# A half tile's matmuls reordered: 16 with the high weights first, 8 with the low weights behind their own wait

## The chip, the core and the metric

The kernel runs on one core of one Trainium2 chip. The metric is the device time of one execution in microseconds; the time of a version is the median of its runs. One further execution was recorded by the hardware profiler, and all rows below come from that one.

## The reference, cut to what matters

One inference step of a decoder layer with 264 tokens (256 of a prompt and 8 single ones), all in float32: a norm, one input projection of 2048 x 7168, convolution and retention heads, an output projection of 2048 x 2048, a second norm, a query projection of 2048 x 2048, a top-16 choice of experts, and then a mixture over all 16384 experts. The two big tables dominate the work:

```python
u = u_tab[idx]
act = jax.nn.gelu(jnp.einsum('td,thkd->thk', xb, u).astype(jnp.float32), approximate=False)
w = (gate * act).astype(xb.dtype)
return jnp.einsum('thk,thkd->td', w, v_tab[idx])
```

The kernel doesn't gather. It multiplies all tokens with the whole of `u_tab` and of `v_tab` and weights each expert by its gate, which is zero for those not chosen.

## The kernel before, in words

**Products in three parts.** Each float32 operand is split into a high part (a cast to the type fp32r) and a low part (the operand less its high part). A product is the sum of three matmuls: high weights with high data, high weights with low data, low weights with high data. The data are 264 columns wide, the tokens.

**Tiles and halves.** All weights are one stream of 344 tiles of 2048 x 128 (in the second table 1024 x 128 pairs), cut into 688 half tiles of 512 KB, each of 8 blocks of 128 x 128. A half tile goes through a ring of 4 slots: SyncE loads it into `raw` (L382), ScalarE casts it to `whi` (L439, semaphore `hi_done`), VectorE subtracts and writes `wlo` (L882, semaphore `lo_done`), and TensorE multiplies in `half` (L629 to L639), 24 matmuls, the last of which counts up `half_used`. SyncE reloads a slot of `raw` when its subtraction is done, and ScalarE casts into a slot of `whi` when TensorE is done with the half tile that was 4 before it.

**The order of the work.** Each engine runs its own list in order, and the lists meet only at semaphores. On ScalarE and VectorE the cast and the subtraction of a tile stand in `ahead(r, k)`, one tile before TensorE's use of it, in among the other work of the stage. The stages are: the first norm (`normalise(0)`, which makes `xhi` and `xlo` two chunks at a time, L921 and L923; TensorE's first tile waits for each two chunks), the heads, the convolution, the output projection, the second norm (`normalise(1)`, the same again), the queries with the top-16 on VectorE (`top16`), the first 8 tiles of `u_tab` (half tiles 176 to 191, beside `route` on VectorE), the gates (batches of 33 small matmuls, L821), and then 16 groups with 16 rounds of 32 half tiles in loops: 8 tiles of `u_tab`, and 8 tiles of `v_tab` with `wexp_hi` and `wexp_lo` as the data.

**What the change and the steps touch.** `half` is called by `tile`, `query_tiles`, `v_tiles` and once for the first tiles of `u_tab`. Its argument `waits` names, for a block c, semaphores that are awaited just before that block's first matmul: after the two norms one wait for each two blocks, for the first output tile one for each block.

Of the kernel before, what the change touches and what calls it, by code (L numbers as in the profile page):

```python
# [41 lines left out]
HALF = 8  # L42
HCOLS = HALF * P
RING = 4
# [118 lines left out]
def build(nc, halves, xT, conv_state, ret_state, norm_mix, conv_w, gn_g, gn_b, norm_ffn, keysT, norm_fin,  # L163
          consts, out_yT, out_conv, out_pret, out_sret):
    with ExitStack() as ctx:
# [3 lines left out]
        def sem(name):  # L169
            return ctx.enter_context(nc.semaphore(name))  # L170
# [137 lines left out]
        hi_done = sem("hi_done")  # L308
        lo_done = sem("lo_done")
# [318 lines left out]
        def _(pe):  # L628
            def half(r, off, out, mh, ml, start, stop, waits=()):  # L629

                s = off % RING
                pe.wait_ge(lo_done, RING * r + off + 1)
                for c in range(HALF):
                    for sem_, need in (waits[c] if c in waits else ()):
                        pe.wait_ge(sem_, need)
                    nc.tensor.matmul(out, whi[:, s, c], mh[c], start=start and c == 0, stop=False)  # L636
                    nc.tensor.matmul(out, whi[:, s, c], ml[c], start=False, stop=False)  # L637
                    mm = nc.tensor.matmul(out, wlo[:, s, c], mh[c], start=False, stop=stop and c == HALF - 1)  # L638
                mm.then_inc(half_used, 1)  # L639

# [6 lines left out]
            def tile(r, k, o4, off, hi_, lo_, waits=({}, {}), between=None):  # L647

                out_free(o4, off)
                b = bank[off % BANKS][:, 0:T]  # L650
                half(r, 2 * k, b, [hi_[:, c, :] for c in range(HALF)], [lo_[:, c, :] for c in range(HALF)],
                     True, False, waits[0])
                if between:
                    between()
                half(r, 2 * k + 1, b, [hi_[:, HALF + c, :] for c in range(HALF)],
                     [lo_[:, HALF + c, :] for c in range(HALF)], False, True, waits[1])
# [113 lines left out]
            def query_tiles(i):  # L770
                first = isinstance(i, int) and i == 0
                for k in range(4):
                    w = norm_waits(CH // 2) if first and k == 0 else ({}, {})
                    if first:
                        pe.wait_ge(x1_ready, CH - BANKS + k + 1)
                    else:
                        pe.wait_ge(q_ready, i * 4 + k - 3)
                    b = bank[k][:, 0:T]
                    r = W_Q // 2 + i * 2
                    half(r, 2 * k, b, [xhi[:, c, :] for c in range(HALF)], [xlo[:, c, :] for c in range(HALF)],  # L780
                         True, False, w[0])
                    if not (first and k == 0):
                        if first and k == 1:
                            pe.wait_ge(keys_in, 32)
                        score(i * 4 + k - 1, (k - 1) % 2)
                    half(r, 2 * k + 1, b, [xhi[:, HALF + c, :] for c in range(HALF)],
                         [xlo[:, HALF + c, :] for c in range(HALF)], False, True, w[1])
# [688 lines left out]
```

## Time and profile before

| | |
|---|---|
| time, median of 3 runs | 2391.52 us (2389.67 to 2396.49) |
| span of the profiled execution, first to last instruction | 2386.3 us |
| median less span | 5.2 us |
| TensorE busy | 2227.3 us |
| matmuls | 20233, of which 16512 in `half` |
| mean granted TensorE clock | 0.963 |

The profiled execution has no time of its own beside its span; the 5.2 us are what lies around the span if it was an execution like the median one. A span is read as a chain: what ended last, and what each piece of it waited for. A matmul's recorded duration overlaps its neighbours', so the pace of TensorE is read from one start to the next.

### The profile page before, as it was taken

What the parts mean: (1) busy time and instruction counts of PE and PEld (TensorE: products, weight loads), DVE (VectorE), ACT (ScalarE), POOL (GpSimd) and SP (SyncE); (2) the same over time, 40 slices, a digit from 0 to 9 for tenths busy, and PEclk for the clock granted to TensorE, in tenths of its full rate; (3) what the DMA queues carried; (4) which work ended last, traced back from release to release, by engine and by line L of the source; (5) the groups of instructions that cost most, each with busy time, mean ns of one, the idle gap of its engine ahead of it and who ended that gap; (6) DMA issues with size and microseconds to landing.
All of it is one profiled execution on the core that took longest, in us unless ns stands there. A gap on an engine that the chain in (4) does not pass through costs nothing.

```text
span 2386.3 us, 52677 instructions
## 1 busy us (share of the span) xinstructions
PE 2227.3 (93%) x20233; PEld 2180.7 (91%) x20233; DVE 1521.5 (64%) x2851; ACT 914.4 (38%) x1162; POOL 33.6 (1%) x55
## 2 busy tenths in 40 slices
PE   4999999997983699999999999999999999999987
PEld 3999899997983699999999999999999999999987
DVE  4566666547789866666666666666666665655554
ACT  2444433332431334344443444434344443333422
POOL 0000000000010000000000000000000000000000
PEclk8999999998996699999999999999999999999999
DMA  3555445553441154545555455454544544555543
GB/s 143 183 171 170 158 151 181 193 174 106 157 135 62 42 171 169 172 165 169 169 168 170 167 169 168 167 171 165 163 168 168 172 165 168 185 179 183 181 135 107
DMA packets 104180, 379.70 MB, mean 159 GB/s; under 512 B 12192, under 2 KB 12464, under 8 KB 103760
## 3 DMA queue, kind: packets, MB, share of 16 engines
q1 hardware_dynamic: 100368, 365.28, 45.9%
q0 software_dynamic: 3648, 11.87, 1.7%
q8 instruction: 148, 2.42, 0.4%
q14 instruction: 16, 0.13, 0.0%
HBM read 370.06 MB, written 6.96 MB: 158 GB/s over the span
## 4 chain that ended last, share of the span: by engine, by line
PE 64%; DVE 5%; issue 2%; DVEq 0%; ACT 0%; ACTq 0%
PE bank L636 21%; PE bank L637 20%; PE bank L638 20%; PE bank L821 3%; DVE gated L1323 1%; DVE wlo L882 1%; DVE gates L1188 1%; DVE gates L1186 0%; DVE acc L1401 0%; PE bank L660 0%; DVE gates L1116 0%; DVE gates L1107 0%; DVE gates L1176 0%; DVE gates L1108 0%; DVE onehot L1314 0%
## 5 line engine op out<-in xcount | busy, mean ns | idle before, releaser
L882 DVE TENSOR_TENSOR wlo<-raw,whi 128x1024 fp32r<-128x1024 f32 x688 | 831.7, 1223 | 656.7 <-ACT whi L439 650.8
L439 ACT CAST whi<-raw 128x1024 fp32r<-128x1024 f32 x688 | 713.1, 1049 | 953.1 <-PE bank L638 931.5
L636 PE MATMUL bank<-xhi,whi 128*128 128x264 f32 x3200 | 928.7, 290 | 48.2 <-DVE xlo L923 21.2
L637 PE MATMUL bank<-xlo,whi 128*128 128x264 f32 x3200 | 914.9, 286 | 0.0
L638 PE MATMUL bank<-xhi,wlo 128*128 128x264 f32 x3200 | 914.5, 286 | 0.0
L636 PEld LDWEIGHTS bank<-xhi,whi 128*128 128x128 f32 x3200 | 610.6, 191 | 65.1 <-issue 50.3
L637 PEld LDWEIGHTS bank<-xlo,whi 128*128 128x128 f32 x3200 | 611.6, 191 | 0.3
L638 PEld LDWEIGHTS bank<-xhi,wlo 128*128 128x128 f32 x3200 | 608.5, 190 | 0.0
L636 PE MATMUL bank<-wexp_hi,whi 128*128 128x264 f32 x2048 | 586.0, 286 | 9.8 <-DVE wexp_lo L1352 9.8
L638 PE MATMUL bank<-wexp_hi,wlo 128*128 128x264 f32 x2048 | 581.6, 284 | 0.0
L637 PE MATMUL bank<-wexp_lo,whi 128*128 128x264 f32 x2048 | 581.0, 284 | 0.0
L636 PEld LDWEIGHTS bank<-wexp_hi,whi 128*128 128x128 f32 x2048 | 386.3, 189 | 10.1 <-issue 9.9
L637 PEld LDWEIGHTS bank<-wexp_lo,whi 128*128 128x128 f32 x2048 | 386.9, 189 | 0.2
L638 PEld LDWEIGHTS bank<-wexp_hi,wlo 128*128 128x128 f32 x2048 | 385.3, 188 | 0.0
L1358 DVE TENSOR_TENSOR acc<-bank,acc 128x264 f32<-128x264 f32 x256 | 100.0, 426 | 68.3 <-PE bank L638 68.3
L821 PE MATMUL bank<-gated,onehot 128*128 128x32 bf16 x3168 | 96.7, 179 | 29.3 <-DVE gated L1323 29.3
L821 PEld LDWEIGHTS bank<-gated,onehot 128*128 128x128 bf16 x3168 | 87.1, 98 | 35.4 <-DVE gated L1323 18.0
L1314 DVE TENSOR_TENSOR onehot<-iota,i2T 128x1408 bf16<-128x1408 bf16 x96 | 84.9, 885 | 0.0
L1323 DVE TENSOR_TENSOR gated<-onehot,stats 128x352 bf16<-128x352 bf16 x288 | 80.6, 335 | 0.0
L636 PE MATMUL bank<-yhi,whi 128*128 128x264 f32 x256 | 75.6, 295 | 0.0
L594 ACT COPY gates<-bank 128x352 f32 x96 | 45.2, 471 | 74.1 <-PE bank L821 74.1
L638 PE MATMUL bank<-yhi,wlo 128*128 128x264 f32 x256 | 72.6, 283 | 0.0
(168 smaller groups left out, 1139.7 us busy)
## 6 DMA issues: line engine op xcount, KB each, us to landing
raw<-halves SPq DMA_DIRECT2D x688, 512.0 KB, 3.3
s_old<-ret_state POOLq DMA_DIRECT2D x8, 512.0 KB, 6.3
ret_sample<-s_new POOLq DMA_DIRECT2D x8, 512.0 KB, 4.1
acc<-xT SPq DMA_DIRECT2D x4, 528.0 KB, 10.8
yT<-acc SPq DMA_DIRECT2D x4, 528.0 KB, 2.6
tables<-shape_constants POOLq DMA_DIRECT2D x1, 1584.0 KB, 8.6
gates<-keysT POOLq DMA_DIRECT2D x1, 1024.0 KB, 5.9
ret_prompt<-state POOLq DMA_DIRECT2D x8, 64.0 KB, 2.7
```

What stands on the lines that cost most here:

```text
L439: nc.scalar.copy(whi[:, s], raw[:, s]).then_inc(hi_done, 1)
L594: nc.scalar.copy(gates[:, q % 2, :, tokens_of(b)], src).then_inc(gb_out, 1)
L636: nc.tensor.matmul(out, whi[:, s, c], mh[c], start=start and c == 0, stop=False)
L637: nc.tensor.matmul(out, whi[:, s, c], ml[c], start=False, stop=False)
L638: mm = nc.tensor.matmul(out, wlo[:, s, c], mh[c], start=False, stop=stop and c == HALF - 1)
L821: mm = nc.tensor.matmul(o, onehot2[:, e, t], gated1[:, e, part, t], start=part == 0, stop=part == PARTS - 1)
L882: v.tensor_tensor(wlo[:, s], raw[:, s], whi[:, s].bitcast(F32), ALU.subtract).then_inc(lo_done, 1)
L1188: ch.did(v.tensor_reduce(out, view(marked), AX.X, ALU.add))
L1314: return v.tensor_tensor(out.rearrange("p t (a d) -> p t a d", d=2), ids.rearrange("p (a d) -> p a d", d=2).unsqueeze(1).to_broadcast(shap ...
L1323: last = v.tensor_tensor(gated1[:, e, part].rearrange("p t (a d) -> p t a d", d=2), onehot1[:].rearrange("p t (a d) -> p t a d", d=2), gat ...
L1358: v.tensor_tensor(acc[:, j, :], bank[off % BANKS][:, 0:T], acc[:, j, :], ALU.add)\
```

## The change

In `half`, the loop over the 8 blocks is parted in two. The first loop waits for `hi_done` (the cast) and issues the two matmuls with `whi` of each block, 16 in all. Then comes the wait for `lo_done` (the subtraction), and a second loop issues the 8 matmuls with `wlo`. The number of matmuls, their operands, the waits in `waits` and the semaphore of the last one are the same; there is one wait more per half tile.

```diff
                 s = off % RING
-                pe.wait_ge(lo_done, RING * r + off + 1)
+                pe.wait_ge(hi_done, RING * r + off + 1)
                 for c in range(HALF):
                     for sem_, need in (waits[c] if c in waits else ()):
                         pe.wait_ge(sem_, need)
                     nc.tensor.matmul(out, whi[:, s, c], mh[c], start=start and c == 0, stop=False)
                     nc.tensor.matmul(out, whi[:, s, c], ml[c], start=False, stop=False)
+                pe.wait_ge(lo_done, RING * r + off + 1)
+                for c in range(HALF):
                     mm = nc.tensor.matmul(out, wlo[:, s, c], mh[c], start=False, stop=stop and c == HALF - 1)
                 mm.then_inc(half_used, 1)
```

## Rows read from the trace of the kernel before

**Rows 1.** The page's busy time, share of the span and instructions of three engines.
```profile
PE 2227.3 (93%) x20233; PEld 2180.7 (91%) x20233; DVE 1521.5 (64%) x2851; ACT 914.4 (38%) x1162; POOL 33.6 (1%) x55
```
**Rows 2.** The page's chain that ended last, share of the span by engine.
```profile
PE 64%; DVE 5%; issue 2%; DVEq 0%; ACT 0%; ACTq 0%
```
**Rows 3.** Waits of PE, whole span: line, releaser: us in total, times, longest.
```profile
PE bank L810 <- DVE gates L1285: 29.9, 1, 29.9
PE bank L821 <- DVE gated L1323: 29.3, 24, 5.6
PE bank L636 <- DVE xlo L923: 21.2, 16, 6.8
...
PE bank L636 <- issue: 15.3, 10, 1.9
PE bank L636 <- DVE wlo L882: 11.6, 3, 7.7
```
**Rows 4.** PE's timeline where a half tile ends: start us, us, line, what.
```profile
1572.57 0.28 PE L637 MATMUL bank<-xlo,whi 128*128 128x264 f32 x1
1572.69 0.28 PE L638 MATMUL bank<-xhi,wlo 128*128 128x264 f32 x1
1572.81 0.28 PE L636 MATMUL bank<-wexp_hi,whi 128*128 128x264 f32 x1
```
**Rows 5.** A piece of the chain: start us, us, a batch of 33 small matmuls.
```profile
832.34 0.83 PE bank L821 x33
```
**Rows 6.** PE's timeline in the first half tile, fourth pair of blocks, and the next.
```profile
46.07 0.59 PE L636 MATMUL bank<-xhi,whi 128*128 128x264 f32 x1 [0.46 <-DVE xlo L923]
...
48.31 0.56 PE L636 MATMUL bank<-xhi,whi 128*128 128x264 f32 x1 [0.55 <-DVE xlo L923]
```
**Rows 7.** PE's timeline, end of the second half tile and start of the third.
```profile
54.65 0.59 PE L636 MATMUL bank<-xhi,whi 128*128 128x264 f32 x1 [0.46 <-DVE xlo L923]
55.04 0.42 PE L637 MATMUL bank<-xlo,whi 128*128 128x264 f32 x1
...
55.92 0.42 PE L638 MATMUL bank<-xhi,wlo 128*128 128x264 f32 x1
56.14 0.42 PE L636 MATMUL bank<-xhi,whi 128*128 128x264 f32 x1
...
57.45 0.28 PE L636 MATMUL bank<-xhi,whi 128*128 128x264 f32 x1
```
**Rows 8.** VectorE's timeline there: the next tile's two subtractions.
```profile
54.51 2.36 DVE L882 TENSOR_TENSOR wlo<-raw,whi 128x1024 fp32r<-128x1024 f32 x2
```
**Rows 9.** PE's timeline, the last pair of blocks after the second norm.
```profile
570.48 0.59 PE L636 MATMUL bank<-xhi,whi 128*128 128x264 f32 x1 [0.46 <-DVE xlo L923]
```
**Rows 10.** PE's timeline, start of half tile 66, in the convolution's first tiles.
```profile
313.28 0.28 PE L638 MATMUL bank<-xhi,wlo 128*128 128x264 f32 x1
313.70 0.39 PE L636 MATMUL bank<-xhi,whi 128*128 128x264 f32 x1
```
**Rows 11.** PE's timeline, start of half tile 180, in the first expert tiles.
```profile
686.93 0.28 PE L638 MATMUL bank<-xhi,wlo 128*128 128x264 f32 x1
694.88 0.56 PE L636 MATMUL bank<-xhi,whi 128*128 128x264 f32 x1 [7.67 <-DVE wlo L882]
```
**Rows 12.** All waits of VectorE from 676 to 762 us.
```profile
DVE gates L1251 <- DVE gates L1116: 0.9, 6, 0.2
DVE wlo L882 <- issue: 0.7, 2, 0.4
```
**Rows 13.** PE's timeline at the start of a round, half tile 256.
```profile
1021.52 0.39 PE L636 MATMUL bank<-xhi,whi 128*128 128x264 f32 x1 [1.99 <-DVE wlo L882]
```
**Rows 14.** VectorE's timeline before and at that start.
```profile
1013.90 1.23 DVE L882 TENSOR_TENSOR wlo<-raw,whi 128x1024 fp32r<-128x1024 f32 x1 [1.67 <-ACT whi L439]
...
1020.19 2.36 DVE L882 TENSOR_TENSOR wlo<-raw,whi 128x1024 fp32r<-128x1024 f32 x2 [0.19 <-issue]
```
**Rows 15.** A window after a round's start: length, busy us and counts, granted clock.
```profile
1624.20:1627.60 3.40, 3.40 (x16) 3.40 (x16) 3.29 (x7) 0.00 (x0) 0.00 (x0) 0.51 0.54 171
```

## The prediction

> **What bounds the kernel now.** I read the busy times first. TensorE computes for 2227.3 of 2386.3 us, VectorE for 1521.5 and ScalarE for 914.4 [rows 1]: the reader is to see that one engine fills 93% of the span and that the two that prepare the weights have room. The chain of waits says the same of the end: TensorE's pieces are by far its largest share, VectorE's 5% [rows 2]. So a change of order inside TensorE's list can only give back what TensorE idles, some 159 us, and of that only the part that it waits for the subtraction. The table of TensorE's waits splits the idle time [rows 3]: 29.9 us for the gates, 29.3 us for the batches' operands, 21.2 us for the low part of the normalised data, 15.3 us for nothing that the profile shows, and for `wlo` 11.6 us, in 3 places, one of them 7.7 us. The 11.6 us, half a per cent of the span, are all that the table offers this change, and each place has to be looked at, since the longest is in a stage where VectorE may be the bound.
>
> Then the pace. Where one half tile ends and the next begins, at the switch from `xhi` to `wexp_hi`, the starts are 1572.57, 1572.69 and 1572.81: 0.12 us from matmul to matmul, across the border as inside a half tile [rows 4]. There the first matmul has the wait for `lo_done`, the one for its bank and the one for `w_ready` before it, all met. I call 0.12 us the pace at full clock.
>
> **Part 1, one more wait per half tile: 0 us.** 688 waits are added, each in the middle of a half tile, and behind it stand only the 8 low matmuls and then the next half tile. A met wait of the same kind costs nothing that two decimals show [rows 4]. If an unseen 2 ns stood behind the rounding, 688 x 0.002 = 1.4 us; that is my upper bound, the lower one is 0, since a wait can't shorten anything. I take 0, the nearest row. The cover for it is that TensorE's list is read much faster than the array needs it: a batch's 33 small matmuls, each with its own weight load, take 0.83 us, 25 ns each [rows 5], against 120 ns for a big one, so some 95 ns are free at each for register work and a wait. Without that cover, an added wait would cost on the scale of those 25 ns, 688 x 0.025 = 17 us.
>
> The Trainium skill has a rule that could speak against this. The page "TensorE: Matmul & The Clock Gate", section "Step-by-step: what each phase is for", says that TensorE pulls a weight load ahead of matmuls in flight; a wait in front of a load is a place where that could stop, and by such a reading every half tile would show a lost overlap. The trace agrees with the pull-ahead and not with a loss at a met wait, the 0.12 us of rows 4.
>
> **Part 2, the low matmuls moved behind the high ones where data come in pieces: +0.7 us twice.** After a norm VectorE delivers `xlo` for two blocks at a time. In the first half tile the fourth pair starts at 46.07 and the next half tile's first pair at 48.31 [rows 6]; the clock is at its lower level, 1.2 GHz: 56.14 - 55.92 = 0.22 us per matmul, 0.39 us from the first after a wait to the second [rows 7]. Before, a pair is 6 matmuls, 0.39 + 5 x 0.22 = 1.49 us, and TensorE idles 0.46 us for the next. After it is 4 matmuls, 1.05 us, and the 8 low ones stand behind the fourth pair. For the first half tile: 46.07 + 1.05 + 8 x 0.22 = 48.88, some 0.57 us past 48.31; the next pair then ends near 48.88 + 0.88 = 49.76, before the one after it is ready (about two and a bit us behind 48.31), so this is absorbed. For the second half tile nothing absorbs it: its last pair starts at 54.65, and behind it now stand 12 matmuls instead of 6. The work left when the last data arrive grows by 6 matmuls. The clock's rise comes near 57.45, where a matmul's recorded duration falls from 0.42 to 0.28 us, in the middle of it, and from 54.65 on TensorE works without a break in both orders, so the same number of matmuls is done at the low clock and the 6 are paid at full clock: 6 x 0.12 = +0.73 us (6 x 0.22 = 1.3 us if the clock stays low longer; with a rise one such stretch later, some 3.4 us at half pace, 1.7 us more). The weights aren't late: VectorE's next subtractions run from 54.51 to 56.87 and the first of them is done before 56.14 [rows 8]. After the second norm the last pair starts at 570.48 with the same 0.46 us of idle [rows 9], and the sum is the same: +0.73 us. Behind both, TensorE is busy without a gap for over 200 us of heads, and for the queries, so I let both reach the end. The first output tile also waits by block, but with no stall: it begins in step behind the tile before it, so nothing there changes.
>
> **Part 3, the wait for the subtraction where it is real: -0.3 us.** Half tile 66 starts at 313.70, 0.42 us after its predecessor's last matmul instead of 0.12 [rows 10]; its cast had been done long before. After, its 16 high matmuls start 0.30 us earlier and cover the subtraction: -0.30 us, and TensorE is the bound behind it.
>
> Half tile 180 is the 7.7 us wait. Its predecessor's last matmul starts at 686.93, it starts at 694.88 [rows 11]. After, the 16 high matmuls run in the wait, from 687.05 for 1.9 us, and 8 are left at 694.88. They and 181 fall into a low-clock stretch in both orders, so what is saved is 16 matmuls at full clock, 16 x 0.12 = 1.9 us, and TensorE finishes this stage 1.9 us earlier. But then it waits 29.9 us for the gates' indices [rows 3], and VectorE, which makes them, waits in all of 676 to 762 us for 1.6 us, none of it for a cast or for TensorE [rows 12]. So what is late next is VectorE with its own work, and the gain turns into 1.9 us more of the 29.9. On the path it is worth 0, with bounds of 0 and -1.9.
>
> **Part 4, the two other waits that the table gives to `wlo`: 0 us.** They are the starts of two rounds. At 1021.52 the table blames VectorE [rows 13]. But the subtractions alternate with the half tiles, every 2.90 us, about three ahead of use: one begins at 1013.90, and the next two, which begin at 1020.19, belong to later half tiles [rows 14]; the one that TensorE needs at 1021.52 is the one before, done some 6 us or more ahead. These idles are of the kind that elsewhere is put down to issue (15.3 us in 10 places, [rows 3]): at a loop's turn TensorE's list runs empty. The new order issues nothing sooner there. Elsewhere in the rounds the subtraction is as far ahead, and the release of a slot hangs on the 24th matmul in both orders, so casts, subtractions and loads keep their times.
>
> **The sum.** +0.73 + 0.73 - 0.30 + 0 + 0 + 0 = +1.2 us on a span of 2386.3, so 2387.5; with the 5.2 us between this execution's span and the median, 2392.7 us. What this kernel's measurement can't tell from no change is about 0.3%, 7.2 us.
>
> **What may move it more.** At two of the rounds' starts the clock falls behind the idle stretch, to 0.51 for 3.4 us [rows 15]: 15 matmuls at 0.22 instead of 0.12, 1.5 us each. Other starts with nearly the same idle have none, so I take it to depend on how the idle lies to the chip's own rhythm, and the number may be anything from none (-3 us) to a handful (+5 us) in either kernel; the spread of the three runs, 6.8 us, is of that size.
>
> The same page has, in "A second HAM failure mode: psum-queue depth-cycling", the rule that many short idles between groups of matmuls make the clock go back and forth. Its effect would fall on the two norms, where idles grow from 0.46 to some 0.9 us per pair; the trace has the clock at its lower level there already, so by this rule, too, only the rise at the end can move.
>
> **Rivals.**
> A, the forecast: 2392.7 us. Chance 0.81.
> B, faster: the idles at the rounds' starts are real waits for the subtraction, as the table says of two of them. Then the 15.3 us and the 11.6 - 7.7 = 3.9 us that are not half tile 180's, 19 us in all, could shrink, as the 16 high matmuls (1.9 us) fit into each: 2391.5 - 19 = 2372 us. For it speaks the releaser named; against it the distance of the subtractions [rows 14] and that most such idles are put down to issue. 0.03.
> C, slower: the wait in the middle of a half tile holds back the weight load behind it. Its price where a wait was really open is seen at half tile 66 (0.39 us long instead of 0.28): 0.11 us, and 688 x 0.11 = 76 us, 2467 us. It decides from 10.5 ns per wait on (7.2 us). Against it stands rows 4. 0.04.
> D, the clock: later rises behind the norms (2 x 1.7 us) and two or three more falls at rounds' starts: up to 2392.7 + 3.4 + 4.5 = 2400.6 us. For it: rows 15; against it: nothing in the change lengthens those idles. 0.05.
> E, half tile 180's time reaches the end: 2392.7 - 1.9 = 2390.8 us. Against it rows 12. 0.07.
>
> **Chances.** Faster by over 0.3% (under 2384.3): B, and a little of A with luck in the clock: 0.04. Slower by over 0.3% (above 2398.7): C, part of D: 0.06. Within: 0.90. The range that should hold 8 in 10 runs from 2389.0 (E with fewer falls of the clock) to 2397.0 (A with three falls more).
>
> **What would show it.** In the trace after: starts still 0.12 us apart at the new wait (part 1); 12 matmuls behind the last `xlo` of each norm and no stall of the third half tile (part 2); half tile 66 at 313.7 - 0.3 + 0.7, the wait for `wlo` of 7.7 us cut to about 5.8 and moved into the middle of half tile 180, and the wait at L810 longer by about 2 (part 3); the rounds 100 us long as before, with 1.6 to 2 us idle at their starts (part 4). The prediction is wrong if the pace at the new wait is not 0.12, if rounds' starts close up, or if a round's length changes by more than 0.1 us outside of the clock.

## The result, and the profile after

The changed kernel takes 2406.2 us (median of 5 runs, 2405.24 to 2409.81), the kernel before 2390.8 in the same session: 15.4 us more by the medians, a ratio of 1.006 with a 95% interval of 1.0043 to 1.0077. Forecast was no change, 2392.7 us. It is slower, and outside of the range.

The page's busy line and chain by engine, after, answer to [rows 1, 2]:

```profile
PE 2244.2 (93%) x20233; PEld 2198.9 (91%) x20233; DVE 1521.6 (63%) x2851; ACT 913.9 (38%) x1162; POOL 33.5 (1%) x55
...
PE 79%; DVE 6%; issue 1%; ACT 1%; DVEq 0%; DMA 0%; POOL 0%; ACTq 0%
```

TensorE has the same 20233 matmuls and is busy 16.9 us longer, of the 22.0 us between the two profiled spans; VectorE and ScalarE are unchanged. So most of the time isn't in waits. TensorE's waits after (engine and line, releaser: us in total, times, longest), to be held against [rows 3]:

```profile
PE bank L812 <- DVE gates L1287: 31.1, 1, 31.1
PE bank L823 <- DVE gated L1325: 29.2, 24, 5.6
PE bank L636 <- DVE xlo L925: 24.8, 14, 6.8
...
PE bank L636 <- ACT whi L439: 17.9, 10, 2.1
...
PE bank L640 <- DVE wlo L884: 7.2, 1, 7.2
```

Nearly the same idle times stand there as before, 5.1 us more in all (22.0 less 16.9), most of it while `xlo` arrives behind the norms (24.8 for 21.2 us), the rest at the gates and at the rounds' starts. Those at the rounds' starts are now put down to the cast, where they were put down to issue or to the subtraction: the name changed with the wait that the first matmul has, and the idle stayed.

The windows from 330 to 430 us lie within the convolution's tiles, where nothing but half tiles runs. First the kernel before, then the one after (length, then busy us and count of PE, PEld, DVE, ACT, POOL, then the granted clock):

```profile
330.00:430.00 100.00, 100.00 (x830) 100.00 (x829) 60.44 (x114) 37.84 (x41) 0.00 (x0) 1.00 0.55 179
```

```profile
330.00:430.00 100.00, 100.00 (x822) 100.00 (x821) 59.54 (x115) 37.08 (x41) 0.00 (x0) 1.00 0.57 181
```

Both are 100% busy at full clock, and after there are 8 matmuls fewer in the same 100 us, 1%. From the start of a half tile to the start of the next it was 2900 ns in 45 of 46 cases of this stage (half tiles 66 to 111, before the output projection), and is 2926 or 2927 ns in all 46. In the rounds an undisturbed half tile (no other matmuls beside it) was mostly 2900 ns, and is mostly 2927 or 2926 with the first table and 2920 with the second. No single matmul shows it. Starts of TensorE in a half tile of the changed kernel:

```profile
357.33 0.29 PE L636 MATMUL bank<-xhi,whi 128*128 128x264 f32 x1
357.46 0.29 PE L637 MATMUL bank<-xlo,whi 128*128 128x264 f32 x1
357.58 0.29 PE L636 MATMUL bank<-xhi,whi 128*128 128x264 f32 x1
357.71 0.29 PE L637 MATMUL bank<-xlo,whi 128*128 128x264 f32 x1
...
358.20 0.28 PE L637 MATMUL bank<-xlo,whi 128*128 128x264 f32 x1
358.32 1.13 PE L640 MATMUL bank<-xhi,wlo 128*128 128x264 f32 x8
359.29 0.28 PE L636 MATMUL bank<-xhi,whi 128*128 128x264 f32 x1
```

The step over the new wait, 358.20 to 358.32, is 0.12 us. The 8 low matmuls take 0.97 us, 121 ns each. Among the 16 in front there are longer steps: the three from 357.33 to 357.71 take 0.38 us, not 0.36.

Where the 22.0 us between the two profiled spans (2386.3 and 2408.3) are, from the starts of half tiles in both traces: up to the fifth half tile 1.0 us (the first norm's last data came 0.9 earlier, and what stands behind them took 1.9 longer); heads 1.0; the wait ahead of half tile 66, 0.3 less; half tile 66 to 144 (convolution and output) 1.9; the four half tiles behind the second norm 1.3; queries 0.9; the first expert tiles and the gates 1.7, which I didn't follow up; half tile 192 to 672, 15 of the 16 rounds, 1496.5 to 1510.6 us, 14.1, of which 3.4 are two falls of the clock more (4 instead of 2, each some 3.4 us at half pace) and 1.0 is longer idles at the rounds' starts; the last 16 half tiles 0.6. That is 22.2 with each piece rounded. Pace is 1.0 + 1.9 + 0.9 in the stages up to the queries and 14.1 - 3.4 - 1.0 = 9.7 in the rounds, some 13.5 us. The medians' 15.4 us are this and the norms, as far as one profiled execution of each tells.

### The profile page after: what moved, and what is told of

Read it like the earlier page. It is cut to its first block, busy times and chain, and to the rows that moved or that the text cites. A ratio compares the mean times of both kernels' runs of the same rounds, so it can differ in the third digit from the quotient of the medians.

```text
span 2408.3 us, 52677 instructions
## 1 busy us (share of the span) xinstructions
PE 2244.2 (93%) x20233; PEld 2198.9 (91%) x20233; DVE 1521.6 (63%) x2851; ACT 913.9 (38%) x1162; POOL 33.5 (1%) x55
## 3 DMA queue, kind: packets, MB, share of 16 engines
q8 instruction: 148, 2.42, 0.4%
## 4 chain that ended last, share of the span: by engine, by line
PE 79%; DVE 6%; issue 1%; ACT 1%; DVEq 0%; DMA 0%; POOL 0%; ACTq 0%
PE bank L636 25%; PE bank L637 25%; PE bank L640 25%; PE bank L823 3%; DVE gated L1325 1%; DVE gates L1190 1%; PE bank L768 1%; ACT whi L439 0%; DVE wlo L884 0%; DVE gates L1188 0%; DVE pair L918 0%; PE bank L751 0%; DVE acc L1403 0%; PE bank L662 0%; DVE xlo L925 0%
## 5 line engine op out<-in xcount | busy, mean ns | idle before, releaser
L636 PE MATMUL bank<-xhi,whi 128*128 128x264 f32 x3200 | 824.8, 292 | 45.1 <-DVE xlo L925 24.8
L637 PE MATMUL bank<-xlo,whi 128*128 128x264 f32 x3200 | 813.0, 288 | 0.0
L636 PE MATMUL bank<-wexp_hi,whi 128*128 128x264 f32 x2048 | 514.3, 287 | 9.8 <-DVE wexp_lo L1354 9.8
L637 PE MATMUL bank<-wexp_lo,whi 128*128 128x264 f32 x2048 | 510.4, 285 | 0.0
L640 PE MATMUL bank<-xhi,wlo 128*128 128x264 f32 x3200 | 458.3, 286 | 7.2 <-DVE wlo L884 7.2
L640 PEld LDWEIGHTS bank<-xhi,wlo 128*128 128x128 f32 x3200 | 419.1, 191 | 7.5 <-DVE wlo L884 7.5
L636 PEld LDWEIGHTS bank<-wexp_hi,whi 128*128 128x128 f32 x2048 | 385.9, 188 | 10.1 <-issue 9.9
L640 PE MATMUL bank<-wexp_hi,wlo 128*128 128x264 f32 x2048 | 291.5, 284 | 0.0
L640 PEld LDWEIGHTS bank<-wexp_hi,wlo 128*128 128x128 f32 x2048 | 268.7, 189 | 0.0
L636 PE MATMUL bank<-yhi,whi 128*128 128x264 f32 x256 | 66.5, 296 | 0.0
L453 ACT ACTIVATE pair<-acc 128x264 f32<-128x264 f32 (+1 forms) x48 | 20.2, 424 | 115.9 <-DVE acc L1088 64.9
```

## The experiments

Theories at the start: WAIT, an added wait costs wherever it stands; MIDDLE, it costs in the middle of a half tile; ORDER, the sequence of the operands sets the pace. Each ratio below is to the kernel before, timed in the same session.

**e1, two waits at the front, order as before.**
```diff
+                pe.wait_ge(hi_done, RING * r + off + 1)
                 pe.wait_ge(lo_done, RING * r + off + 1)
```


> Matmul order as before; each half tile's first matmul waits for the cast and for the subtraction (688 waits more, none in the middle of a half tile). Theory WAIT (an added wait costs the 20 to 27 ns that each half tile has grown by, wherever it stands): 2400 to 2408 us, an undisturbed half tile of about 2920 ns from start to start. Theory MIDDLE (only a wait in the middle costs, since it stops the pull-ahead of the weight load) and theory ORDER (the sequence of operands costs): 2391 us, half tile 2900 ns as before.

Measured: 2433.5 us, ratio 1.0171 (1.0147 to 1.0195), and yet 2900 ns per half tile. All theories missed the time; the pace speaks against WAIT for half tiles in the stream. What costs is another thing, at the rounds' starts. TensorE's timeline at one of them:

```profile
1023.84 0.36 PE L637 MATMUL bank<-xhi,whi 128*128 128x264 f32 x1 [2.02 <-DVE wlo L883]
...
1026.89 0.28 PE L639 MATMUL bank<-xhi,wlo 128*128 128x264 f32 x1 [1.85 <-issue]
```

Where [rows 13] had one idle, there are two, the second ahead of the half tile's ninth matmul. The second wait didn't go onto the matmul that has the first: the trace has 651 separate semaphore instructions of TensorE's sequencer more (787 for 136), and the instruction queue moved more:

```profile
q8 instruction: 167, 2.74, 0.4%
```

(148 packets and 2.42 MB before). The second idle comes 11 times, 0.96 to 2.15 us, 19.3 us in all or 18.0 beyond 11 ordinary steps; the idles at the half tiles' own starts are 9.1 us longer, two new ones included; and the clock is at its lower level for 54.6 us of the rounds instead of 6.8, which costs up to 24 us (nothing where TensorE idles anyway). That is up to 51 us, and from half tile 192 to 672 this kernel takes 45.0 us more than the one before. Why the second idle comes isn't shown.

**e2, the order alone, with the old wait.**
```diff
                 pe.wait_ge(lo_done, RING * r + off + 1)
                 for c in range(HALF):
@@
                     nc.tensor.matmul(out, whi[:, s, c], ml[c], start=False, stop=False)
+                for c in range(HALF):
                     mm = nc.tensor.matmul(out, wlo[:, s, c], mh[c], start=False, stop=stop and c == HALF - 1)
```


> Order of the changed kernel (16 with the high weights, then 8 with the low), but only the old wait for the subtraction ahead of the half tile. Theory ORDER: still 2920 to 2927 ns per half tile, and 2404 to 2408 us. Theories WAIT and MIDDLE: 2900 ns per half tile; about 2392.5 us, since the 6 matmuls behind each norm's last data stay (+1.5 us).

Measured: 2406.6 us, 1.0065 (1.0043 to 1.0086); 2927 and 2920 ns. The whole loss without the change's wait. In the window of above:

```profile
330.00:430.00 100.00, 100.00 (x822) 100.00 (x821) 60.43 (x114) 37.90 (x42) 0.00 (x0) 1.00 0.55 175
```

**e3, a wait in the middle alone.**
```diff
+                    if c == 5:
+                        pe.wait_ge(lo_done, RING * r + off + 1)
                     mm = nc.tensor.matmul(out, wlo[:, s, c], mh[c], start=False, stop=stop and c == HALF - 1)
```


> Order as before; besides the wait at the start, the wait for the subtraction stands a second time before the 18th matmul (the low one of block 5), where it is always met. Theories WAIT and MIDDLE: 2920 ns per half tile or more, 2402 to 2408 us. Theory ORDER: 2900 ns and 2391 us.

Measured: 2395.1 us, 1.0001 (0.9986 to 1.0015), 2900 ns. The middle wait alone costs nothing, and the order alone costs all (e2): WAIT and MIDDLE are out, ORDER stands.

**e5, another order: three passes.**
```diff
                     nc.tensor.matmul(out, whi[:, s, c], mh[c], start=start and c == 0, stop=False)
+                for c in range(HALF):
                     nc.tensor.matmul(out, whi[:, s, c], ml[c], start=False, stop=False)
+                for c in range(HALF):
                     mm = nc.tensor.matmul(out, wlo[:, s, c], mh[c], start=False, stop=stop and c == HALF - 1)
```


> Only the old wait, and another order: the 8 matmuls of high weights and high data, then the 8 of high weights and low data, then the 8 of low weights. Theory ORDER says that the pace depends on which operands follow each other, so this must differ from 2900 ns per half tile too, I expect 2915 to 2950 ns, 2400 to 2425 us. Theories WAIT and MIDDLE: 2900 ns, 2392 to 2394 us (behind each norm's last data stand 18 matmuls or so).

Measured: 2397.3 us, 1.0023 (1.0011 to 1.0034), and against my expectation 2900 ns per half tile in the long stages. Its 5.5 us (by the ratio) are not pace: with 18 matmuls behind each norm's last data, from these to the fifth half tile of the stage it takes 10.5 and 11.7 us, where the kernels with the old order take 7.9 and 9.0 on average, 5.3 us more in all. What is told of the pace is in the steps from start to start (ns, the first being the step to the half tile's first matmul; medians over the convolution's half tiles, most of which agree within 1 ns in these two kernels):

```
three passes   126 121 120 122 121 115 120 122 | 126 121 120 121 121 116 119 123 | 126 120 120 122 121 116 119 122
after          126 121 126 123 123 122 121 121 116 127 127 125 122 126 118 121 | 122 121 121 122 121 116 119 122
```

The pattern of the three passes repeats with the 8 blocks, whichever weights and whichever of the two data tensors are in use. And with `wexp_hi`, which lies elsewhere in memory, the same pattern is there turned by three places (116 119 122 126 121 120 122 121). The changed kernel's low pass is the last third of it. That pointed to the address of the data. The rows of the blocks are 264 x 4 = 1056 bytes apart. The new theories: ADDRESS, the pace depends on where the data begin and how that goes from matmul to matmul; WEIGHT, the same weights loaded twice running cost; TENSOR, going to and fro between high and low data costs.

**x1, all matmuls of a half tile read its first block's data** (the data of the other 7 are left out).
```diff
-                    nc.tensor.matmul(out, whi[:, s, c], mh[c], start=start and c == 0, stop=False)
-                    nc.tensor.matmul(out, whi[:, s, c], ml[c], start=False, stop=False)
-                    mm = nc.tensor.matmul(out, wlo[:, s, c], mh[c], start=False, stop=stop and c == HALF - 1)
+                    nc.tensor.matmul(out, whi[:, s, c], mh[0], start=start and c == 0, stop=False)
+                    nc.tensor.matmul(out, whi[:, s, c], ml[0], start=False, stop=False)
+                    mm = nc.tensor.matmul(out, wlo[:, s, c], mh[0], start=False, stop=stop and c == HALF - 1)
```


> Leaves the data of blocks 1 to 7 out: every matmul of a half tile reads the data of block 0, so all begin at the same address of their tensor; order, weights and waits are those of the kernel before. Theory ADDRESS (the pace depends on where the 1056 bytes of data begin, since the rows of the blocks lie 1056 bytes apart, and how that goes from one matmul to the next): the half tile is no longer 2900 ns, I expect less, 2700 to 2850 ns, and 2200 to 2360 us. Theories WEIGHT (the same weights loaded twice running cost something) and TENSOR (going to and fro between the high and the low data costs something): 2900 ns and 2391 us, since both go on as before.

Measured: 2393.0 us, 0.9991 (0.9974 to 1.0007). The gain that I expected isn't there: 2907 to 2918 ns in the convolution's half tiles, 2920 in most of the second table's, 2880 in some of the others. The median of each step over the convolution's half tiles is 121 ns, which looks like even steps and isn't: single half tiles show a pattern of five matmuls, which begins at another place in each. Steps of four half tiles (ns):

```
68, convolution    120 121 126 124 116 120 121 125 125 115 120 121 126 124 116 120 121 126 124 116 120 121 125 125
184, first table   120 120 120 120 120 120 120 120 120 120 120 120 120 120 120 120 120 120 120 120 120 120 120 120
230, first table   117 123 117 123 117 123 117 123 117 123 117 123 117 123 117 123 117 123 117 123 117 123 117 123
209, second table  122 122 121 122 122 121 122 122 121 122 122 121 122 122 121 122 122 121 122 122 121 122 122 121
```

The first three have the same instructions, and data at the same addresses in every matmul of a kind. So uneven steps come without changing addresses too, and one sequence of addresses has more than one pace, 120.0 or 121.4 ns on average. In this trace a pace that had settled went on until a pause, other matmuls or another data tensor came between. The pattern of the 8 blocks is gone, though the weights still go through them: it isn't the weights' addresses that made it.

**x5, other weights on the changed kernel's data.**
```diff
                     nc.tensor.matmul(out, whi[:, s, c], mh[c], start=start and c == 0, stop=False)
-                    nc.tensor.matmul(out, whi[:, s, c], ml[c], start=False, stop=False)
-                    mm = nc.tensor.matmul(out, wlo[:, s, c], mh[c], start=False, stop=stop and c == HALF - 1)
+                    nc.tensor.matmul(out, wlo[:, s, c], mh[c], start=False, stop=False)
+                for c in range(HALF):
+                    mm = nc.tensor.matmul(out, whi[:, s, c], ml[c], start=False, stop=stop and c == HALF - 1)
```


> Two passes as in the changed kernel, but the first pass has per block high weights, then low weights, both with the high data, and the second pass has the high weights with the low data; one wait at the start. The data begin at the same places in their tensors, matmul by matmul, as in the changed kernel. ADDRESS: 2927 and 2920 ns as there, 2406 us. WEIGHT and TENSOR: 2900 ns and 2392.5 us, as no weights come twice running and the tensors don't alternate.

Measured: 2404.7 us, 1.0057 (1.0034 to 1.0081); 2927 and 2920 ns, and the 24 steps of the convolution's half tiles are those of the line "after" above, each to the nanosecond, though no weights come twice running and the first 16 matmuls use only `xhi`. The same stretch as above, 0.18 us later in this kernel:

```profile
357.51 0.29 PE L636 MATMUL bank<-xhi,whi 128*128 128x264 f32 x1
357.64 0.29 PE L637 MATMUL bank<-xhi,wlo 128*128 128x264 f32 x1
357.77 0.29 PE L636 MATMUL bank<-xhi,whi 128*128 128x264 f32 x1
357.89 0.29 PE L637 MATMUL bank<-xhi,wlo 128*128 128x264 f32 x1
...
358.50 1.13 PE L639 MATMUL bank<-xlo,whi 128*128 128x264 f32 x8
359.47 0.28 PE L636 MATMUL bank<-xhi,whi 128*128 128x264 f32 x1
```

WEIGHT and TENSOR fall, as far as whole tensors go; where the data lie within them is the same, matmul by matmul.

**x4 and x6, the old order with the blocks in another sequence.**
```diff
-                for c in range(HALF):
+                for c in (range(HALF) if waits else (0, 2, 4, 6, 1, 3, 5, 7)):     # x4
+                for c in (range(HALF) if waits else (0, 4, 1, 5, 2, 6, 3, 7)):     # x6
```


> The kernel before with the blocks taken as 0, 2, 4, 6, 1, 3, 5, 7 in half tiles that don't wait by block. ADDRESS: another length of the half tile than 2900 ns, anywhere from 2860 to 2940. WEIGHT and TENSOR: 2900 ns, 2391 us.

> The kernel before with the blocks taken as 0, 4, 1, 5, 2, 6, 3, 7 in half tiles that don't wait by block. ADDRESS: a length other than 2900 ns and other than with steps of two, 2860 to 2940. WEIGHT and TENSOR: 2900 ns, 2391 us.

Measured: x4 2398.7 us, 1.004 (1.0024 to 1.0056), 2912 to 2915 ns. x6 2401.9 us, 1.0043 (1.0031 to 1.0055), 2907 ns with the first table and 2941 to 2945 ns with the second. ADDRESS said only that the lengths would change, and they do. In these two the weights' blocks change their sequence with the data's.

**x10 and x12, 128 unused bytes between the high and the low data**, in the changed kernel (x10) and in the one before (x12), with not an instruction moved. `xhi` and the weights, which are allocated ahead of the gap, stay; `xlo` and all behind it, `wexp_hi` and `wexp_lo` among them, move by 128 bytes (by the order of allocation in the kernel; the traces have no addresses).
```diff
+        gap = sb("gap", [P, 32])
         xlo = sb("xlo", [P, CH, T], F32R)
```


> The changed kernel, with 128 unused bytes between the high and the low data, so that the low data of a block begin 128 bytes further round than the high ones; the instructions are the same. ADDRESS: the half tiles of all stages but the second table leave 2927 ns, to anywhere in 2880 to 2950. If it is the order of the instructions alone that costs: 2927 and 2920 ns, 2406 us.

> The kernel before with the same 128 unused bytes. ADDRESS: half tiles leave 2900 ns, to anywhere in 2880 to 2950 (each 10 ns is 7 us if it holds everywhere). If the order of the instructions alone decides: 2900 ns, 2391 us.

Measured: x10 2403.1 us, 1.0048 (1.0032 to 1.0064), 2920 ns where it was 2927 and 2913 or 2914 where it was 2920. x12 2398.5 us, 1.0031 (1.0019 to 1.0044), 2904 or 2923 ns in the stages with `xhi`, still 2900 with the second table, whose high and low data keep their distance. The window from 330 us, x10 and then x12 (before 830, after 822):

```profile
330.00:430.00 100.00, 100.00 (x824) 100.00 (x823) 59.73 (x115) 37.85 (x41) 0.00 (x0) 1.00 0.56 179
```

```profile
330.00:430.00 100.00, 100.00 (x827) 100.00 (x825) 60.05 (x114) 37.88 (x41) 0.00 (x0) 1.00 0.54 179
```

The placement alone changes the pace. The single steps say more (ns, medians, the convolution of the changed kernel and of x10, then the second table of the kernel before and of x12):

```
after    126 121 126 123 123 122 121 121 116 127 127 125 122 126 118 121 | 122 121 121 122 121 116 119 122
x10      126 121 121 122 123 128 117 120 120 125 116 124 122 120 123 125 | 124 121 122 122 121 115 120 122

before   120 124 122 122 118 120 122 129 120 122 121 116 | 120 121 123 119 123 122 121 119 120 118 118 120
x12      120 121 123 119 123 122 121 118 120 118 118 120 | 120 124 122 122 118 120 122 129 120 122 121 116
```

In x10 the 16 matmuls that go to and fro between `xhi` and the moved `xlo` have other steps, and the 8 behind them, with `xhi` alone, keep theirs within 2 ns. In x12 both data tensors of the second table moved together, and its pattern is the old one turned by 12 matmuls, four blocks, within 1 ns: that is why it keeps its 2900 ns. Four blocks are 4 x 1056 = 16 x 256 + 128 bytes, so there the place within 256 bytes would be enough to tell the step. It isn't the whole rule: in x12's convolution the two half tiles of a tile, whose data begin 8 x 1056 = 33 x 256 bytes apart, take 2923 and 2904 ns in turn. x12's time also holds 7 falls of the clock in its profile instead of 2.

**x9, the changed order in the second table's 256 half tiles only, one wait.**
```diff
+                if v_half:       # True from v_tiles: 16 with whi, then 8 with wlo
+                    ...
+                else:            # as before
+                    ...
```


> The changed kernel's order in the 256 half tiles of the second table only, one wait at the start everywhere. ADDRESS: 2920 ns in those, 2900 in all others, so 256 x 20 ns = +5.1 us, 2396 to 2397 us. If the slowdown came from elsewhere in the changed kernel (the norms, the clock), nothing or all of it.

Measured: 2394.4 us, 1.0025 (1.001 to 1.004), which is +6.0 us (2.4 to 9.6) for 5.1 expected; 2920 ns in those half tiles, 2900 in the others. From half tile 192 to 672 it takes 4.7 us more than the kernel before, with 2 falls of the clock in either. The medians of the executions differ by 2.3 us only (2394.4 and 2392.1), so it is the half tiles, more than the time, that show that the loss goes with the count.

**x7, the change's purpose with a sequence that keeps the pace.**
```diff
-                pe.wait_ge(lo_done, RING * r + off + 1)
+                pe.wait_ge(lo_done if waits else hi_done, RING * r + off + 1)
+                if waits:        # by block: as before
+                    ...
+                else:
+                    for c in range(HALF):
+                        nc.tensor.matmul(out, whi[:, s, c], mh[c], start=start and c == 0, stop=False)
+                    for c in range(HALF):
+                        nc.tensor.matmul(out, whi[:, s, c], ml[c], start=False, stop=False)
+                    pe.wait_ge(lo_done, RING * r + off + 1)
+                    for c in range(HALF):
+                        mm = nc.tensor.matmul(out, wlo[:, s, c], mh[c], start=False, stop=stop and c == HALF - 1)
```


> The purpose of the change with another order: in half tiles that don't wait by block, 8 matmuls of high weights and high data, 8 of high weights and low data, both behind the cast alone, then the wait for the subtraction and the 8 with the low weights; half tiles that wait by block stay as in the kernel before. Theory ADDRESS with a free wait: 2900 ns per half tile in the long stages, no longer work behind the norms, half tile 66 0.3 us earlier: 2388 to 2392 us, not to be told from the kernel before. If the wait in the middle costs after all together with an order that leaves the block's own sequence, 2920 ns and 2403 us or more.

Measured: 2388.0 us, 0.9995 (0.9982 to 1.0008), 2900 ns. 16 matmuls lead on the cast alone, the wait for the subtraction stands in the middle, and nothing is lost; nothing that can be measured is won either. Its wait at half tile 180 and the one for the gates:

```profile
PE bank L819 <- DVE gates L1294: 31.9, 1, 31.9
...
PE bank L647 <- DVE wlo L891: 5.6, 1, 5.6
```

7.7 + 29.9 = 37.6 before, 5.6 + 31.9 = 37.5 now.

## Why the prediction was wrong, point by point

**The step that failed** is not one of the terms but one that the sum lacks: it took the 24 matmuls, since they are the same in number and operands, to take the same time in any order. I read the pace as 0.12 us in two decimals [rows 4]. The loss is 20 to 27 ns per half tile, 0.8 to 1.1 ns per matmul, and times 16512 that is 14 to 19 us. Two decimals can't show it; the length of a half tile (24 matmuls, 2900 against 2920 to 2927 ns) or the count in a fixed window can. The prediction's own sign of being wrong came true: outside of the clock a round takes 0.7 us more, (14.1 - 3.4) / 15, where it allowed 0.1. e2 shows that the order does it, x5 that it isn't the weights, and x10 and x12, with x5, that it is where the data lie. Why one sequence of places is slower than another stays open, and x1 shows that the places alone don't fix the pace. The rivals had no such mechanism. C had the right sign, with five times the size and the wrong cause; D had it too, up to 2400.6 us, and its clock did add some in the profile (3.4 us), but not the most.

**Part 1, the wait: 0.** Right for a wait on a matmul that has none (e3, x7, and 358.20 to 358.32 above). e1 shows the bound that I hadn't seen: a second wait on one matmul becomes an instruction of its own, and the kernel with 651 of these takes 42 us more, nearly all of it in the rounds and with the idles and the clock there. The change isn't touched by it; its instruction count is the same 52677.

**Part 2, the norms: +0.73 us twice.** The mechanism is there. The last pair, then the 8 low matmuls and the next half tile, after:

```profile
53.79 0.59 PE L636 MATMUL bank<-xhi,whi 128*128 128x264 f32 x1 [1.29 <-DVE xlo L925]
...
54.84 1.96 PE L640 MATMUL bank<-xhi,wlo 128*128 128x264 f32 x8
56.59 0.42 PE L636 MATMUL bank<-xhi,whi 128*128 128x264 f32 x1
...
59.01 0.28 PE L637 MATMUL bank<-xlo,whi 128*128 128x264 f32 x1
```

56.59 - 53.79 = 2.80 us for the 1.49 of [rows 7], 1.31 more, which is 6 x 0.22. But the clock rose 5.2 us after the last pair's start, not 2.8, so the 6 weren't paid at full clock, and from the last data to the fifth half tile it is 1.9 us more in the first and 1.3 in the second norm. One pair of executions can't settle the size: kernels with the old order scatter there by over a microsecond, 7.4 to 8.8 us behind the first norm and 8.3 to 9.8 behind the second. The four with the new order (after, e2, x5, x10) take 8.7 to 10.1 and 9.9 to 10.2. By the means it is 1.6 and 1.0 us more, so +0.73 twice was too small, most of all for the first, where the prediction paid the 6 matmuls at full clock.

**Part 3.** Half tile 66 starts at 315.38, 0.12 us after its predecessor's last, and the subtraction it needs ended at 315.93:

```profile
314.71 1.22 DVE L884 TENSOR_TENSOR wlo<-raw,whi 128x1024 fp32r<-128x1024 f32 x1
```

The 0.30 us were won, as forecast. Half tile 180's wait went into its middle and the wait for the gates grew, 7.7 and 29.9 to 7.2 and 31.1, where 5.8 and about 32 were forecast. The wait was cut by less because VectorE was later too: its subtraction ended 9.4 us behind the start of half tile 179's last matmul, for 7.8 before. In other kernels with the old wait half tile 180 starts 7.8 to 9.4 us behind that matmul, so this scatters. x7 has 5.6 and 31.9. Worth 0 on the path, as forecast.

**Part 4.** The idles at the rounds' starts stayed (11 of 1.8 to 2.5 us from start to start, 1.7 to 2.3 before, 1.0 us more in all), under another name. Right.

**The clock.** 4 falls in the rounds' profile instead of 2, 3.4 us. Over all kernels with the old 52677 instructions it was 1 to 7, without a rule that I could find, so I call this one scatter; that it is wasn't tested.

## What to carry to other kernels

Where an engine is over 90% busy with one kind of instruction, its pace is a term of its own: take it from a long window to a tenth of a per cent, in every stage, and treat a new order of the same instructions as a change of it. Before giving a matmul an earlier or later wait, look whether it has one already. And ask what is gained if a wait goes: here 0.3 us were to be had, against 16512 matmuls that were put at risk.

## What the runs showed of the hardware

- Matmuls of 128x264 with fp32r operands start 121 ns apart on average at full clock in the old order; single steps run from 115 to 132 ns in a fixed pattern that repeats within 1 ns. It follows the place in memory of the moving data (x10, x12), not the weights (x5). Sequences and placements of all 8 blocks gave 2900 to 2945 ns per half tile, 1.6%. What about the address does it isn't settled: equal addresses (x1) have patterns of their own, of five matmuls at 121.4 ns on average or of even 120 ns (2880 ns), and which of them comes isn't settled by the addresses. A layout with rows at another distance than 1056 bytes wasn't tried.
- A second wait ahead of one matmul became an instruction of its own and cost nothing in the stream (2900 ns in e1), but at a loop's turn a second idle of 1 to 2 us appeared, and the granted clock fell for 3.4 to 6.8 us at nearly each turn. That the added instructions' loading is behind it is argued from the instruction queue's count, not shown.
- The releaser that a table names at a loop's turn need not be the cause: for the idles there the tables name issue and `wlo` (before), mostly `whi` (after), and mostly `wlo` (e1).
